# First stage of a two-block transformer kernel: two channel pairs taken from the un-normalised input, one sum product, other orders of loads and weight splits

## The reference, cut to what matters

```python
h = rms_norm(x, norm1_g)          # x * rsqrt(mean(x*x) + EPS) * norm1_g
z = h @ w_in
q, k, v, xr, yr, gate_logits = jnp.split(z, IN_SPLITS, axis=-1)
...
rnn = rg_lru(causal_depthwise_conv(xr, conv_w, conv_b), w_rg_a, b_rg_a, w_rg_x, b_rg_x,
             rg_lambda) * jax.nn.gelu(yr)
```

## Time and profile before

| | |
|---|---|
| median of 3 runs | 2972.59 us |
| lowest, highest | 2968.69, 2976.43 us |
| the profiled execution: its time | 2966.75 us |
| the profiled execution: span from first to last instruction | 2964.6 us |
| busy in it: TensorE, VectorE, ScalarE, GpSimd | 2909.5, 1905.4, 1152.0, 847.0 us |
| instructions | 35559 |

### The profile page before, as it was taken

How to read it: one execution, slowest core, us unless ns; L and a number is a source line. 1 busy time by engine, 2 the same in 40 slices (tenths; PEclk the granted TensorE clock), 3 DMA queues, 4 the chain that set the end, 5 groups by cost and what they waited for, 6 DMA issues and landing times.

```text
span 2964.6 us, 35559 instructions
## 1 busy us (share of the span) xinstructions
PE 2909.5 (98%) x13947; PEld 2495.9 (84%) x13947; DVE 1905.4 (64%) x3255; ACT 1152.0 (39%) x1704; POOL 847.0 (29%) x523
## 2 busy tenths in 40 slices
PE   8999999999999999999999999999999999899999
PEld 6877777789889999998999999998888877688887
DVE  6664665578888895426888788875444567644443
ACT  5674655433333334433232232323222356632221
POOL 0000000128788888872323223321000300210000
PEclk9999999999999999999999999999999999999999
DMA  4325564336656676798988888842322321133222
GB/s 147 110 91 210 199 224 167 132 101 139 137 123 141 156 157 143 173 258 321 338 308 307 288 316 318 307 156 93 98 94 93 117 85 50 50 100 100 92 93 71
DMA packets 240807, 489.28 MB, mean 165 GB/s; under 512 B 97664, under 2 KB 149440, under 8 KB 240128
## 3 DMA queue, kind: packets, MB, share of 16 engines
q1 hardware_dynamic: 175680, 417.87, 42.9%
q0 software_dynamic: 64960, 69.14, 10.2%
HBM read 443.18 MB, written 77.23 MB: 176 GB/s over the span
## 4 chain that ended last, share of the span: by engine, by line
PE 80%; DVE 13%; ACT 4%; issue 2%; POOL 1%; DMA 0%; SPq 0%; POOLq 0%; ACTq 0%
PE pb L719 26%; PE pb L721 25%; PE pb L720 25%; DVE whl L1747 2%; ACT scr L1273 2%; DVE ST L1747 1%; DVE S L1747 1%; ACT whl L1276 1%; DVE ST L1755 1%; PE pb L1011 1%; DVE su L1996 1%; DVE ST L1997 1%; DVE su L1999 1%; DVE scr L1747 1%; PE pb L894 1%
## 5 line engine op out<-in xcount | busy, mean ns | idle before, releaser
L719 PE MATMUL pb<-H,whl 128*128 128x512 f32 (+1 forms) x2400 | 939.5, 391 | 6.3 <-ACT scr L1273 2.2
L721 PE MATMUL pb<-H,whl 128*128 128x512 f32 (+1 forms) x2400 | 911.3, 380 | 0.0
L720 PE MATMUL pb<-H,whl 128*128 128x512 f32 (+1 forms) x2400 | 910.7, 379 | 0.0
L1747 DVE TENSOR_TENSOR whl<-raw,whl 128x1024 fp32r<-128x1024 f32 (+5 forms) x554 | 650.2, 1188 | 251.8 <-ACT whl L1276 239.7
L1276 ACT ACTIVATE whl<-raw 128x1024 fp32r<-128x1024 f32 (+5 forms) x554 | 544.8, 1003 | 361.6 <-PE pb L721 360.4
L719 PE MATMUL pb<-S,whl 128*128 128x448 f32 (+2 forms) x1732 | 654.5, 378 | 14.9 <-DVE S L1747 7.7
L721 PE MATMUL pb<-S,whl 128*128 128x448 f32 (+2 forms) x1732 | 649.5, 375 | 0.0
L720 PE MATMUL pb<-S,whl 128*128 128x448 f32 (+2 forms) x1732 | 649.4, 375 | 0.0
L719 PEld LDWEIGHTS pb<-H,whl 128*128 128x128 f32 x2400 | 451.3, 188 | 83.3 <-issue 8.8
L720 PEld LDWEIGHTS pb<-H,whl 128*128 128x128 f32 x2400 | 451.5, 188 | 71.7 <-issue 6.0
L721 PEld LDWEIGHTS pb<-H,whl 128*128 128x128 f32 x2400 | 450.6, 188 | 71.9
(11 more groups left out here) (224 smaller groups left out, 2515.0 us busy)
## 6 DMA issues: line engine op xcount, KB each, us to landing
raw<-in_pu SPq DMA_DIRECT2D x128, 512.0 KB
raw<-in_pv SPq DMA_DIRECT2D x128, 512.0 KB
raw<-in_w_in SPq DMA_DIRECT2D x72, 512.0 KB
ad<-scr SPq DMA_DIRECT2D x128, 224.0 KB
GA<-gd SPq DMA_DIRECT2D x60, 448.0 KB, 4.3
GA<-ad SPq DMA_DIRECT2D x60, 448.0 KB, 6.1
raw<-in_wg SPq DMA_DIRECT2D x44, 512.0 KB
raw<-in_wu SPq DMA_DIRECT2D x44, 512.0 KB
```

What stands on the lines that cost most here:

```text
L719: e.matmul(o, lh, h, start=start, stop=False, skip_group_check=True)
L720: e.matmul(o, lh, l, start=False, stop=False, skip_group_check=True)
L721: return e.matmul(o, ll, h, start=False, stop=stop, skip_group_check=True)
L1747: return e.tensor_tensor(o, x, y, op)
```

## The change

- TensorE: `sums` is removed. Groups 0 and 1 both come from the un-normalised input (`two` twice). In the second, after its k = 0, stands one product of ones with the sum of the squares, which VectorE builds up in scr[0] with seven additions. For d = 2 and 3 the wait before xr is for `xr_scaled`.
- The un-normalised parts lie in another place (g1h, g1l), so that results of groups 0 and 1 don't overwrite them.
- SyncE: X's first quarter, two weight units, X's other quarters, then cst and the rest.
- ScalarE: the table with logarithm and exponential is asked for at the start. High parts of w0 and w1 are made after k = 1, squares are two tiles behind the scaling, w2 and w3 (split up to 3, 4) follow later, w4 before the logarithm, w5 inside the norm.
- VectorE: low parts in the same order; inside the norm stand the scaling of xr 0 and the low parts of w4 and w5; the constants' preparation moves behind the norm.
- In the loop both engines split, for each d, all that is to be had up to unit j + 6 ahead of the copy or the convolution (j is the unit of xr d), where before it was up to j + 3 there and one more behind the convolution.
- Group 1's xr and yr are scaled by VectorE; ScalarE no longer copies xr 1.

```diff
@@ -611,6 +611,7 @@
...
         gh, gl, first_q = oh, ol, (sum_sq, one_sq)
+        g1h, g1l = cut(S_t[:, 1024:5120], 8), cut(S_t[:, 6144:10240], 8)
         o_root = [scr[8]] * 7 + [scr[7]]
@@ -730,10 +731,10 @@
...
-            def two(j, outs, hh, hl, ready, done, tag=None):
+            def two(j, outs, hh, hl, ready, done, tag=None, at_k=4):
                 for k in range(8):
-                    if k == 4 and tag:
+                    if k == at_k and tag:
                         sum_of(tag)
@@ -744,15 +745,13 @@
...
             def sum_of(tag):
-                q.wait_ge(pool, ("sq", tag))
-                e.matmul(bank[7], ones, sum_sq, start=True, stop=True, skip_group_check=True).then_inc(
+                if tag == "1":
+                    q.wait_ge(cst_in, "cst")
+                    q.wait_ge(dve, "sq_sum")
+                else:
+                    q.wait_ge(pool, ("sq", tag))
+                e.matmul(bank[7], ones, scr[0] if tag == "1" else sum_sq, start=True, stop=True, skip_group_check=True).then_inc(
                     prod.up(("sums", tag)), 1)
-
-            def sums(tag, sq, b, lhs=ones):
-                for k, s in enumerate(sq):
-                    q.wait_ge(act, ("sq", tag, k))
-                    last = e.matmul(b, lhs, s, start=k == 0, stop=k == len(sq) - 1, skip_group_check=True)
-                last.then_inc(prod.up(("sums", tag)), 1)
@@ -784,19 +783,18 @@
...
             def recurrence():
-                q.wait_ge(cst_in, "cst")
-                sums("1", scr[0:8], bank[7])
+                g1 = [("g", "1", k) for k in range(8)]
                 for c in range(0, 10, 2):
...
                         i = d % 2
-                        if d == 0:
-                            j = q.unit("w_in", 24)
-                            q.unit("w_in", 34)
-                            two(j, (bank[0], bank[2]), gh, gl, [("g", "1", k) for k in range(8)], (("xr", 0), ("yr", 0)))
+                        if d < 2:
+                            j = q.unit("w_in", 24 + d)
+                            q.unit("w_in", 34 + d)
+                            two(j, (bank[i], bank[2 + i]), g1h, g1l, g1, (("xr", d), ("yr", d)), "1" if d else None, 1)
                             continue
-                        if d == 2:
-                            q.wait_ge(dve, "xr_scaled")
-                        elif d > 2:
+                        if d < 4:
+                            q.wait_ge(dve, ("xr_scaled", d - 2))
+                        else:
                             q.wait_ge(act, ("xr_raw", d - 2))
@@ -1257,7 +1255,8 @@
...
         def scalar(eng, e):
-            q, hi_done, logs = Waits(eng, units), [0], [False]
+            q, hi_done, logs = Waits(eng, units), [0], [True]
+            e.preload_act_table_set("natural_log_exp_and_others")
@@ -1299,10 +1298,11 @@
...
-            def norm(tag, sq, r, b, hi, mid=lambda: None, free=()):
+            def norm(tag, sq, r, b, hi, mid=lambda: None, free=(), between=lambda k: None):
                 mid()
...
                 for k in range(8):
+                    between(k)
                     for signal_, name in free:
@@ -1349,22 +1349,27 @@
...
                 q.wait_ge(prm_in, "prm")
-                for k in range(8):
-                    q.wait_ge(x_in[k // 2], ("x", k // 2))
-                    run(ACT.Square, scr[k], X[k]).then_inc(act.up(("sq", "1", k)), 1)
-                    e.activation(gh[k], X[k], ACT.Copy, scale=prm("norm1_g", k)).then_inc(act.up(("ghi", "1", k)), 1)
+                for k in range(10):
+                    if k < 8:
+                        q.wait_ge(x_in[k // 2], ("x", k // 2))
+                        e.activation(g1h[k], X[k], ACT.Copy, scale=prm("norm1_g", k)).then_inc(act.up(("ghi", "1", k)), 1)
+                    if k == 1:
+                        split(2)
+                    elif k > 1:
+                        run(ACT.Square, scr[k - 2], X[k - 2]).then_inc(act.up(("sq", "1", k - 2)), 1)
                     if k == 5:
-                        split(2)
-                norm("1", scr, scr[8], bank[7], Hh, lambda: split(4))
+                        split(3)
+                    elif k == 7:
+                        split(4)
+                norm("1", scr, scr[8], bank[7], Hh, lambda: split(5), between=lambda k: split(6) if k == 5 else None)
                 for c in range(0, 10, 2):
...
                         i = d % 2
-                        weights("w_in", 24 + d)
-                        if d == 0:
-                            weights("w_in", 34)
-                        if d:
+                        split(q.unit("w_in", 24 + d) + NW + 2)
+                        q.unit("w_in", 34 + d)
+                        if d > 1:
                             q.wait_ge(prod, ("xr", d))
-                            q.wait_ge(dve, ("conv", d - 2) if d > 1 else ("pad0", i))
+                            q.wait_ge(dve, ("conv", d - 2))
                             copy(pad[i][:, 32:544], bank[i]).then_inc(act.up(("xr_raw", d)), 1)
@@ -1372,18 +1377,16 @@
...
                         copy(cvh[d % 4], rhf[d]).then_inc(act.up(("conv_hi", d)), 1)
-                        if d:
-                            weights("w_in", 34 + d)
                         if d == 1:
...
                             run(ACT.Exp, sq[1], sq[1]).then_inc(act.up("softplus_exp"), 1)
-                        if d:
+                        if d > 1:
                             q.wait_ge(prod, ("yr", d))
                         else:
-                            q.wait_ge(dve, "yr_scaled")
-                        run(ACT.Gelu_apprx_tanh, rlf[d], bank[2 + i] if d else rlf[0]).then_inc(act.up(("gelu", d)), 1)
+                            q.wait_ge(dve, ("yr_scaled", d))
+                        run(ACT.Gelu_apprx_tanh, rlf[d], bank[2 + i] if d > 1 else rlf[d]).then_inc(act.up(("gelu", d)), 1)
                     if c:
@@ -1769,9 +1772,10 @@
...
-            def norm(tag, xs, gains, sq, r, hi, lo, mid=lambda: None):
+            def norm(tag, xs, gains, sq, r, hi, lo, mid=lambda: None, between=lambda k: None):
                 mid()
                 for k in range(9):
+                    between(k)
                     if k < 8:
@@ -1809,15 +1813,20 @@
...
+            def scaled_x(c):
+                q.wait_ge(prod, ("xr", c))
+                tt(pad[c][:, 32:544], bank[c], scr[8], ALU.mult).then_inc(dve.up(("xr_scaled", c)), 1)
+
             def conv4(c, beside=()):
                 i, cv, w = c % 2, rhf[c], [prm("conv_w", 4 * c + j) for j in range(4)]
-                if c:
+                if c > 1:
                     q.wait_ge(act, ("xr_raw", c))
                 else:
-                    q.wait_ge(prod, ("xr", 0))
-                    then(tt(pad[0][:, 32:544], bank[0], scr[8], ALU.mult), "xr_scaled")
-                    q.wait_ge(prod, ("yr", 0))
-                    tt(rlf[0], bank[2], scr[8], ALU.mult).then_inc(dve.up("yr_scaled"), 1)
+                    if c:
+                        scaled_x(1)
+                    q.wait_ge(prod, ("yr", c))
+                    tt(rlf[c], bank[2 + c], scr[8], ALU.mult).then_inc(dve.up(("yr_scaled", c)), 1)
+                    q.wait_ge(dve, dve.n)
                 then(ts(cv, pad[i][:, 32:544], w[3], ALU.mult, prm("conv_b", c), ALU.add))
@@ -1852,10 +1861,17 @@
...
                 q.wait_ge(prm_in, "prm")
-                for k in range(8):
-                    gained("1", k, "norm1_g", gh, gl, ("g", "1", k))
-                    if k == 5:
+                for k in range(10):
+                    if k < 8:
+                        gained("1", k, "norm1_g", g1h, g1l, ("g", "1", k))
+                    if k == 1:
                         split(2)
+                    elif k == 8:
+                        split(4)
+                    if k > 2:
+                        q.wait_ge(act, ("sq", "1", k - 2))
+                        then(tt(scr[0], scr[0], scr[k - 2], ALU.add), *(["sq_sum"] if k == 9 else []))
+                norm("1", X, gains("norm1_g"), scr, scr[8], Hh, Hl, between=lambda k: scaled_x(0) if k == 2 else split(5) if k == 4 else split(6) if k == 7 else None)
                 q.wait_ge(cst_in, "cst")
@@ -1864,15 +1880,11 @@
...
                     e.memset(pad[i][:, 0:32], 0.0).then_inc(dve.up(("pad0", i)), 1)
-                norm("1", X, gains("norm1_g"), scr, scr[8], Hh, Hl, lambda: split(4))
                 for c in range(0, 10, 2):
                     for d in (c, c + 1):
-                        weights("w_in", 24 + d)
-                        if d == 0:
-                            weights("w_in", 34)
+                        split(q.unit("w_in", 24 + d) + NW + 2)
+                        q.unit("w_in", 34 + d)
                         conv4(d, (d - 4, d - 3) if d in (4, 6, 8) else ())
-                        if d:
-                            weights("w_in", 34 + d)
                         if d == 1:
@@ -2454,8 +2466,8 @@
...
-            def load_x(name):
```

(8 more changed lines are left out.)

## The result

Over 13 runs of each the changed kernel takes 2974.0 us in the median (2969.48 to 2979.58) and the kernel before 2969.06 (2965.49 to 2976.43): 1.0018 times the time, interval 1.0011 to 1.0025, or 5.3 us (3.3 to 7.4) more; the two medians themselves are 4.9 us apart. It is slower, by less than the 0.3% taken as the bound. The forecast was 4.6 us more; its 2977.2 stood on the 3 runs' median of 2972.59, and with 13 runs that median is 3.5 us lower.

A forecast was written before the change was run, and what follows sets the result against it. TensorE, busy 2909.5 of 2964.6 us, was taken as the bound. Lag 3.1, last round 0.4 and clock 1.1 sum to 4.6 us, which on the 2972.59 median gives 2977.2; range 2966 to 2984.

The forecast's parts named there:

- The head: From the start through the normalisation: TensorE starts at 9.0, and the last H part comes at 39.2 against 33.1.
- the first pair: First two un-normalised groups: TensorE starts at 9.0, ten matmuls at the slow clock and 38 at full, done at 21.9.
- Where the lead goes: Units 36 and 37 wait for gelu 0 and 1: TensorE's 7.8 us lead becomes a lag, 3.1 us at rgate 0.
- The last round: Splits before convolutions 8 and 9 make r_sig 8 0.4 us later still; TensorE resumes at 201.3 against 197.77.
- The clock: The longer idle stretch before r_sig 8 drops TensorE's clock until about 203.5, losing 1.1 us behind 201.3.
- rival C: Slow clock behind the two new idle stretches, or a late start: slower by more than 8.9 us, 2982; chance 0.14.
- The sum: Total over the first stage: 3.1 + 0.4 + 1.1 = 4.6 us slower.
- A: Rival: the side chain keeps up and the 7.8 us head start is kept; 2964.8, or 2959 with all; chance 0.13.
- B: Rival: nothing moves, as an earlier sum of squares and no clock fall leave 2 us or less; 2972 to 2975; 0.20.
- D: Rival: a table load stays in front of the logarithm, adding 1.3 us to the 4.6; chance counted in A and B.

The follow-up runs named there:

- e1: The changed kernel, with TensorE waiting before units 36 and 37 for yr_scaled 0 and 1 instead of gelu 0 and 1; 1.0012 of the kernel before.
- e5: The changed kernel with the splits of groups 8 and 9 placed as in the kernel before; 1.0011 of the kernel before.
- e8: The changed kernel with six unused fp32 ones products in TensorE's idle stretch behind 192 us; 1.0010 of the kernel before.
- e2: e1 plus the lambda scalars taken out of the side chain into VectorE's idle stretches; 0.9996 of the kernel before.
- e3: e2 plus yr 0 scaled right behind the norm, and xr 1 and yr 1 right behind convolution 0; 0.9980 of the kernel before.
- e4: The kernel before with only the change's further-ahead splits in the loop; 1.0003 of the kernel before.
- e6: The changed kernel with the edits of e3 and e5 together; 0.9978 of the kernel before.
- e7: The kernel before with the lambda scalars spread over idle stretches and the first table asked for at the start; 0.9990 of the kernel before.

## Why the prediction was right

*The head.* All of it came as walked: TensorE at 9.0 (9.06), the sum at 23.3 (23.29), the first scaled channel at 25.7 (25.80), the last H part at 39.2 (39.20), unit 26 held by 0.6 (0.51). That it fits to 0.1 us is in part luck: e1, e5 and e8 have the same program up to the sum, and had it at 23.48, 23.07 and 24.53. The prediction's working for the first pair also adds up to 22.3 as it stands (9.0, ten slow matmuls of 0.46 and 38 of 0.23), and not to its 21.9; the trace has nine slow ones in 4.0 us, and 21.93. The seven additions were taken at zero, and are hidden: they end at 22.77, ahead of the product. The table load in front of the logarithm was worth 1.28 us, as the row said: the logarithm now starts 0.04 us behind the product (24.31), where it started 1.32 us behind it. "ScalarE: Activation LUTs" of the Trainium skill (What ACT_TABLE_LOAD costs) has about 2.66 us for a switch, and the trace doesn't agree with it.

*Where the lead goes.* Gelu 0 and unit 36 at 47.4 (47.21), gelu 1 and unit 37 at 61.6 (61.23), rgate 0 at 78.4 (78.26). The lag behind the kernel before was put at 3.1 us from there on; by ScalarE's waits for the second gate of each pair it is 3.0:

```profile
113.90 0.69 ACT L1272 ACTIVATE scr<-pb,prm 128x512 f32<-128x512 f32 x1 [1.30 <-PE pb L722]
...
149.26 0.69 ACT L1272 ACTIVATE scr<-pb,prm 128x512 f32<-128x512 f32 x1 [0.78 <-PE pb L722]
```

(110.89 before, and 35.36 us behind it 146.25 by the same wait.) e1 and e2 show that it is the chain and not one of the waits: take the waits away and rgate 0 has the time; take the scalars out too, and TensorE leads. That the chain starts late because the normalisation ends 6.1 us later is read from the traces (39.20 against 33.10); no run here gives the change an early normalisation.

*The last round.* The lag grew by 0.5 us over the last round (3.5 us at r_sig 8, from 3.0), the forecast said 0.4. e5 is in line with this: with the old splits 0.5 to 0.7 us come back. A small miss: TensorE still waited 0.47 us at 187.10 for a weight part, where no wait was expected; it is hidden too.

*The clock.* Stretches of the changed kernel; the columns are again busy time by engine, granted clock, DMA share and GB/s:

```profile
48.00:50.00 2.00, 2.00 (x7) 1.52 (x6) 1.86 (x2) 1.05 (x2) 0.00 (x0) 0.50 0.00 0
50.00:52.00 2.00, 2.00 (x9) 1.64 (x8) 1.96 (x4) 0.00 (x0) 0.00 (x0) 0.87 0.60 211
...
202.00:204.00 2.00, 2.00 (x6) 1.52 (x5) 1.35 (x2) 2.00 (x4) 0.00 (x0) 0.50 0.96 352
204.00:206.00 2.00, 2.00 (x10) 1.65 (x9) 1.23 (x2) 2.00 (x4) 0.00 (x0) 0.97 0.59 185
```

TensorE works at half speed (the 1.2 GHz level) from 47.2 to about 50.5, and from 198 to about 204. The first was to be covered by 0.5 us; unit 27 was done 1.27 us before gelu 1 came, so the cover was larger and rival C lost its place. The second was put at 1.1 us and measured 1.3 (e8); that it fell as forecast and not as in e2, which lost 0.3 us, the walk could not know. "TensorE: Matmul & The Clock Gate" (HAM oscillation) of the Trainium skill says that such gaps bring the slow clock back. The traces agree in the first stage behind its head, for every idle stretch of 2.85 us and more, and show no fall there behind 1.63, 1.46 and 0.81 us. They don't agree on each time: behind the stage one idle stretch of 3.55 us brought the slow clock in some executions and not in others (the part on what stays open).

*The sum.* 3.1 + 0.4 + 1.1 = 4.6 us was forecast; 3.0 + 0.5 + 1.3 = 4.8 is what the traces have, 4.9 between the two at the attention stage, 5.3 (3.3 to 7.4) in the runs. The runs agree within a wide interval only; it is the traces that test the mechanism.

*The rivals.* A fell at gelu 1; that its gain exists is shown by e3, which keeps 2.3 us of it at the attention stage and more in the runs. B would have needed an earlier sum. D didn't occur.

*What stays open.* The runs and the first stage don't agree in size. In us against the kernel before (the ratio times 2969, and the start of the product with squares against 257.7):

| kernel | runs | first stage |
|---|---|---|
| changed | +5.3 | +4.9 |
| e1_bank_waits | +3.6 | +4.9 |
| e2_scalars_early | -1.2 | +1.2 |
| e3_scalings_early | -5.9 | -2.3 |
| e4_splits_alone | +0.9 | +1.5 |
| e5_last_round | +3.3 | +2.9 |
| e6_all_and_last_round | -6.5 | -5.5 |
| e7_before_scalars_early | -3.0 | -0.5 |
| e8_filled_idle | +3.0 | +4.9 |

Seven of the eight experiments come out better in the runs, by 0.6 to 3.6 us, against a half-width of the interval of 2.7 us. A part of this is the head of the one profiled execution: those of e2, e3, e4, e7 and e8 were 0.6 to 1.5 us late. With that taken off, no experiment differs by more than 2.1 us (e3), and six still come out better; what is left was not traced to a cause.

Behind the first stage the kernels have one program, and the traces show two places where executions of it part. The first is an idle stretch of 3.55 us near 567. Here are the changed kernel, then e1, with the stretch of time behind it (busy time by engine, granted clock, DMA share and GB/s):

```profile
570.91 0.79 PE L720 MATMUL pb<-S,whl 128*128 128x512 f32 x1 [3.55 <-DVE S L1750]
...
572.00:576.00 4.00, 4.00 (x11) 3.12 (x10) 1.58 (x3) 1.61 (x3) 0.42 (x1) 0.50 0.94 333
```

```profile
570.93 0.50 PE L720 MATMUL pb<-S,whl 128*128 128x512 f32 x1 [3.56 <-DVE S L1750]
...
572.00:576.00 4.00, 4.00 (x19) 3.33 (x18) 1.65 (x3) 1.63 (x3) 0.46 (x1) 1.00 0.93 333
```

The clock fell in the changed kernel and in the kernel before, and stayed up in e1, e3 and e4. From the last product with squares to the next ones product it takes 135.6 us in the kernel before (477.3 to 612.9), 135.5 in the changed one (482.2 to 617.7) and 133.1 in e1 (482.2 to 615.3), so the slow clock costs 2.4 us there. The second place is a wait for a weight part in the changed kernel:

```profile
1336.63 0.44 PE L720 MATMUL pb<-H,whl 128*128 128x448 f32 x1 [2.42 <-DVE whl L1750]
```

e2, e6 and e7 have it too (2.61, 2.40 and 1.78 us), e1 has 0.62 us of it, and the kernel before and the others have none; why was not looked into. The runs fit a part for the clock: of the 33 runs of the kernel before in the session of e1, the five with a mean granted clock of 0.997 took 2965.8 us on average, and the five with 0.994 took 2973.5. That is a correlation; no run here sets the clock.

## What to carry to other kernels

A head start for the busiest engine lasts only as far as the slack of the engines that feed it. Before work is moved from it to them, walk their serial chain to the next place where it hands something over, and compare that with the slack that the trace shows (2.3 us here, against 6 us of delay). A removed wait tells little if the same chain is waited for once more behind it, and a visible stall is worth nothing where a later wait swallows it: e5 brought one back, and its stage became shorter. Small dependent steps that stand in such a chain can be spread over stretches in which their engine waits anyway; together with scalings moved out of the chain, that turned a loss of 0.2% into a gain of 0.2% here (the scalars alone only made the loss good: 0.9996).

## What was not expected of the hardware

- The slow pace of TensorE at the start doesn't end at the same time in every execution. The changed kernel and e8 have one program there, and TensorE starts at 9.06 and 9.47; but between 13 and 15 us it did ten matmuls in the one and six in the other, and the ones product started at 23.29 and 24.53. The two stretches, first of the changed kernel, then of e8:

```profile
13.00:15.00 2.00, 2.00 (x10) 1.62 (x10) 1.96 (x4) 1.39 (x3) 0.00 (x0) 1.00 1.04 422
```

```profile
13.00:15.00 2.00, 2.00 (x6) 1.52 (x6) 1.93 (x4) 1.41 (x3) 0.00 (x0) 1.00 1.03 414
```

  The granted clock is given as 1.00 in both, so that the slow pace is read from the count and spacing of the matmuls and not from the clock's record; that it is a slow clock is inferred. e2 and e3 have six there as well, e1, e5 and e6 ten. It is worth about 1 us in the head, and e2's and e3's late heads (0.95 and 1.5 us) are for the most part this; e6, with e3's program up to there, had ten matmuls and a head of 38.41.
- The first quarter of X landed between 5.1 and 6.3 us in ten profiled executions, with the same issue time.
- Six products of no use made the stretch behind them 1.3 us shorter (60.02 against 61.32), with the granted clock at 1.00 all through.
- The same idle stretch of 3.55 us, in the same program, was followed by a granted clock of 0.50 in one execution and of 1.00 in another. One trace doesn't show whether a gap costs clock.
